# A hybrid attention and expert layer: mixed heads transposed before the addition of x1, squares of x1 behind the copies of its transpose, zero rows of the biases written later

## What is computed

```
h = rms_norm(x, g_attn);  proj = h @ w_in
y_a = sparse attention, 8 heads of 64, over the 128 keys that an indexer picks
y_b = differential attention, 4 heads of 128, each normalised and scaled
x1  = x + concat(y_a, y_b) @ w_o
h2  = rms_norm(x1, g_ffn)
out = x1 + moe(h2)      # 4 of 32 experts for each token: gate/up, clamped SwiGLU, down
```

## Time and profile before

| | |
|---|---|
| time, median of 3 runs | 1516.82 us (1516.62 to 1521.65) |
| time of the profiled execution | 1517.85 us |
| its span, first to last instruction | 1515.7 us |
| mean granted clock of TensorE | 0.985 |
| PE busy | 1455.6 us, 96% |
| DVE busy | 1313.3 us, 87% |
| ACT busy | 1106.0 us, 73% |
| POOL busy | 235.3 us, 16% |

### The profile page before, as it was taken

The page is one execution under the profiler, slowest core; times in us unless marked ns, Lnnn a source line. Parts: engine busy times, 40 slices in busy tenths (PEclk is TensorE's granted clock), DMA queues, the critical chain, the costliest instruction groups (busy, mean ns, idle before and its releaser), DMA issues.

```text
span 1515.7 us, 18818 instructions
## 1 busy us (share of the span) xinstructions
PE 1455.6 (96%) x7145; PEld 1197.8 (79%) x7148; DVE 1313.3 (87%) x1320; ACT 1106.0 (73%) x1197; POOL 235.3 (16%) x120
## 2 busy tenths in 40 slices
PE   6999888989999999999999999999999999999996
PEld 5887767776788888888888888888888888888885
DVE  5799776548799999999999999999999999999995
ACT  6666554445777787788877787888778778887773
POOL 1222000011111111211111112111111221111101
PEclk9999979999999999999999999999999999999998
DMA  5422111168999999999999999999999999999991
GB/s 159 139 70 56 42 43 42 45 245 314 334 366 359 373 370 369 363 378 364 369 367 376 367 372 368 375 371 364 356 369 374 361 371 368 368 367 363 382 362 34
DMA packets 102308, 448.53 MB, mean 296 GB/s; under 512 B 18497, under 2 KB 23617, under 8 KB 69377
## 3 DMA queue, kind: packets, MB, share of 16 engines
q1 hardware_dynamic: 89808, 428.32, 73.1%
q0 software_dynamic: 9792, 18.90, 5.1%
q10 hardware_dynamic: 2608, 0.01, 0.1%
HBM read 440.89 MB, written 23.07 MB: 306 GB/s over the span
## 4 chain that ended last, share of the span: by engine, by line
PE 84%; DVE 10%; ACT 2%; issue 2%; DMA 1%; POOL 1%; ACTq 0%; POOLq 0%; DVEq 0%
PE ps L1950 68%; PE ps L1712 2%; PE ps L1714 2%; PE ps L1713 2%; PE ps L1960 2%; PE ps L1919 2%; PE ps L1724 2%; PE ps L1911 2%; DVE work L1390 1%; DVE top L1389 1%; DVE nmax L1401 1%; PE ps L1815 1%; DVE W L570 1%; DMA out_dram<-ysb 1%; PE ps L1786 0%
## 5 line engine op out<-in xcount | busy, mean ns | idle before, releaser
L775 DVE TENSOR_TENSOR whl<-wraw,whl 128x2048 fp32r<-128x2048 f32 x384 | 865.8, 2288 | 84.5 <-ACT whl L770 77.7
L770 ACT ACTIVATE whl<-wraw 128x2048 fp32r<-128x2048 f32 x384 | 732.7, 1918 | 208.2 <-PE ps L1950 208.2
L1950 PE MATMUL ps<-whl,xT 128*128 128x512 f32 x3120 | 732.1, 392 | 1.6 <-issue 1.3
L1950 PEld LDWEIGHTS ps<-whl,xT 128*128 128x128 f32 x3120 | 581.7, 188 | 123.5 <-issue 2.0
L1950 PE MATMUL ps<-whl,aT 128*128 128x512 f32 x1488 | 346.1, 391 | 0.4 <-DVE whl L775 0.4
L1950 PEld LDWEIGHTS ps<-whl,aT 128*128 128x128 f32 x1488 | 276.9, 188 | 56.8 <-DVE whl L775 0.8
L939 POOL DMA_INDIRECT out_dram<-ysb,idx x32 | 100.3, 3135 | 453.6 <-ACT ysb L1224 440.2
L930 POOL DMA_INDIRECT xg<-h_rows,idx x32 | 88.4, 2762 | 471.2 <-DVE idx L1608 463.5
L1712 PE MATMUL ps<-W,HT 128*128 128x512 f32 (+1 forms) x184 | 71.9, 391 | 5.4 <-DVE W L570 4.4
L1714 PE MATMUL ps<-W,HT 128*128 128x512 f32 (+1 forms) x184 | 68.9, 374 | 0.0
L1713 PE MATMUL ps<-W,HT 128*128 128x512 f32 (+1 forms) x184 | 68.6, 373 | 0.0
(11 more groups left out here) (248 smaller groups left out, 1363.0 us busy)
## 6 DMA issues: line engine op xcount, KB each, us to landing
wraw<-in_w_gu_dram SPq DMA_DIRECT2D x256, 1024.0 KB, 8.0
wraw<-in_w_down_dram SPq DMA_DIRECT2D x128, 1024.0 KB, 7.2
WR<-in_w_in_dram SPq DMA_DIRECT2D x20, 512.0 KB, 3.7
WR<-in_w_o_dram SPq DMA_DIRECT2D x8, 512.0 KB, 3.7
xs<-in_x_dram SPq DMA_DIRECT2D x4, 512.0 KB, 7.8
WR<-in_x_dram SPq DMA_DIRECT2D x4, 512.0 KB, 3.6
out_dram<-WR SPq DMA_DIRECT2D x4, 512.0 KB, 2.6
h_rows<-WR SPq DMA_DIRECT2D x4, 512.0 KB, 2.6
```

Source lines behind the costliest of these rows:

```text
L770: act.activation(whl[:, n % HL, 0, :], wraw[n % RAW], ACT.Copy).then_inc(chunk_hi, 1)
L775: eng.tensor_tensor(whl[:, n % HL, 1, :], wraw[n % RAW], whl[:, n % HL, 0, :].bitcast(F32), ALU.subtract).then_inc(chunk_lo, 1)
L1950: ins = pe.matmul(bank, a[x_][j], w[:, b, j, 512 * q:512 * q + 512], start=c == NG and j == 0 and n == 0, stop=last and j == nj - 1 and n ...
```

## The change

Three things are altered. In the plan, both `turn_y` steps of tile 1 move from the end of unit 40 to the end of unit 39, ahead of `post(0)`; `turn_y(2, 1)` moves from unit 50 to unit 49, ahead of `post(1)`; and in unit 59 `post(2)` comes before `mix_b(3)`. On ACT the squares of x1 of tiles 0 to 2 move from `post` behind the copy in `turn_x1`. On POOL the zeros of the biases wait until both engines have read the bank of `turn_y(3, 1)`.

```
-        35: [("mix_b", 1)], 37: [("mix_scale", 1)], 40: [("turn_y", 1, 0), ("turn_y", 1, 1)],
-        44: [("mix_b", 2)], 46: [("mix_scale", 2)], 50: [("turn_y", 2, 1), ("mix_a", 2)], 53: [("turn_y", 2, 0)],
+        35: [("mix_b", 1)], 37: [("mix_scale", 1)], 39: [("turn_y", 1, 0), ("turn_y", 1, 1)],
+        44: [("mix_b", 2)], 46: [("mix_scale", 2)], 49: [("turn_y", 2, 1)], 50: [("mix_a", 2)], 53: [("turn_y", 2, 0)],
...
+LATE[59].reverse()
...
                 elif st[0] == "biases":
                     pool.wait_ge(score_ps, SCORE["all"])
+                    wait_turns(pool, through(("turn_y", T - 1, 1)))
...
                 elif kind == "post":
-                    t = st[1]
-                    if t < T - 1:
-                        act.wait_ge(x1_ok, t + 1)
-                        act.activation(h2, x1, ACT.Square, accum_out=tss[:, 0:1]).then_inc(x1_sq, 1)
+                    continue
                 elif kind == "turn_x1":
...
-                    if t == T - 1:
-                        act.wait_ge(x1_ok, T + 1)
-                        act.activation(h2, x1, ACT.Square, accum_out=tss[:, 0:1]).then_inc(x1_sq, 1)
+                    act.wait_ge(x1_ok, t + 1 if t < T - 1 else T + 1)
+                    act.activation(h2, x1, ACT.Square, accum_out=tss[:, 0:1]).then_inc(x1_sq, 1)
```

## The result

The changed kernel took 1511.26 us (median of 8 runs, 1509.66 to 1514.02). The kernel before, run again beside it, took 1519.9 us (8 runs, 1516.51 to 1524.14). The ratio is 0.9944, with a 95% interval of 0.9934 to 0.9955: 8.5 us, 0.56% less. The time lies 3.3 us above the forecast of 1508.0 and inside its range, close to its upper end. The gain itself, 8.5 us with an interval of 6.8 to 10.0, is 1 us short of the forecast sum of 9.5.

A forecast was written before the change was run, and what follows sets the result against it. TensorE is full in the experts, so its waits from 225 to 345 us and the half clock after them bound the gain. 2.45 + 0.2 + 2.65 + 2.5 + 1.7 = 9.5 us, forecast 1508.0 us, range 1505.5 to 1512.5.

The forecast's parts named there:

- Units 39 and 40: Heads of tile 1, x1 of tile 0: earlier transposes and out projection, with clock returning, give 2.45 us; bounds 0.75 to 2.6.
- rival (a): Clock gives nothing back after the pause before x1 of tile 0: 6.1 us remain, 1510.7; chance 0.25.
- Units 49 to 51: Tile 2's heads, x1 of tile 1: the wait only changes its name, 0.2 us; bounds 0.5 lost to 0.6 gained.
- Unit 59 and the squares: x1 of tile 2: earlier addition and later squares start the second half of transposes 2.65 us sooner; bounds 0.85 and 2.65.
- Rival (b): Only the zeros count; DVE's hold in `post_mean` and tile 1's late addition eat the rest: 4.2 us, 1512.6; chance 0.10.
- The zeros: Routing of tile 2: moving POOL's MEMSET frees DVE's held CAST and gives 2.5 us; bounds 2.2 and 2.5.
- The clock behind it: After the last out projection's shortened pause, half clock vanishes, giving 1.7 us; bounds 0 and 1.7.
- The base: Starting time of the forecast: profiled execution 1517.85 us, median of runs 1516.82; results 1508.3 and 1507.3, 1508.0 taken.
- Slower (c): After split pauses in units 39 to 41 the clock stays at 1.2 GHz, costing 12 us, 1519.5; chance 0.03.
- no effect (d): The moved MEMSET meets another row of DVE, at most 2.65 us; chance 0.04 together with others.

The follow-up runs named there:

- the kernel with the search put off: The changed kernel with DVE's top-k pairs of units 39 and 40 put off to the end of the search: 1508.86 us, ratio 0.9925.
- the kernel with the half head put back: The changed kernel with `turn_y(2, 1)` back in unit 50, behind the addition of x1 of tile 1: 1508.97 us, ratio 0.9929.
- all but the heads: The kernel before with the zeros later, unit 59 turned round and the squares behind the copies, without the moved `turn_y` steps: 1512.2 us, ratio 0.9948.
- the kernel with all three edits: The changed kernel with tile 1's `turn_y` in unit 38, top-k pairs of units 39 and 40 put off, `turn_y(2, 1)` back in unit 50: 1506.57 us, ratio 0.9907.

## Why the prediction came out as it did

**Units 39 and 40: the mechanism right, one part of the term wrong.** It had three parts. PE's transposes of x1 start sooner: the wait is named after the addition, as predicted. They were to start 2.4 us sooner and did so by 2.5 (237.61 less the 1.79 us lost ahead of unit 38 is 235.82, against 238.30). `turn_p` waits for DVE's copy and the out projection starts 1.5 us sooner: 241.85 less 1.79 is 240.06, 1.45 us. And then "if the clock is full again by then, [...] another 0.95". The clock was at half for as long and until as late as before, and of the 1.45 us 0.68 were left at unit 48. The bound that the prediction gave for this, "only the work that fits into 1.5 us of half clock is ahead, 0.75", is what happened; the term was 0.7 and not 2.45. The failed step is the reason given for the choice, "since PE now has work from 235.9 on instead of 238.3". That work is short, and the pause ahead of it is still 3.1 us, followed by a second of 1.7. The kernel with seven idle matmuls shows that the fall followed the first of them. That one and the kernel with the search put off, in which the first or the second pause was cut, had 3.4 us at half clock each; so both pauses seem to have a part in the 6.9 us. This was rival (a), for this stretch.

**Units 49 to 51: the sum right, its parts opposite.** 0.16 us against 0.2 predicted, and the wait did change its name. But the squares alone and the kernel with the half head put back show that the moved `turn_y` loses 0.27 us and that the squares give 0.43. The prediction reckoned only the sum of the links and did not see that the edit without the move would have been better.

**Unit 59 and the squares: right.** 2.55 us against 2.65, half from each edit (1.28 by the squares alone, 1.27 as the difference). DVE was held in `post_mean` for 1.77 us, 1.8 predicted, the row maximum behind it ran at 304.85, and no wait of PE followed from it. Rival (b), which let this hold eat the gain and leave 4.2 us, a ratio of 0.9972, is refuted by all but the heads, 0.9948 with an interval that ends at 0.9962.

**The zeros: right.** 2.49 us against 2.5, the CAST 0.17 us, PE's pause 1.07 against 1.3. The CAST took 2.67 us in all four traces that have the MEMSET beside it, and 0.17 in all ten that don't. At the new place the MEMSET, 2.66 us from 313.59, met no row of DVE: the last had ended at 313.38 and the next began at 318.70. The page SBUF — State Buffer of the Trainium skill, in its section Who interferes with whom, says that a cast on VectorE and an instruction on GpSimd can exclude each other on a shared port pair, the later one for the whole of the earlier. The trace agrees: both started within 0.01 us and ended within 0.03. That it is the port, no run here shows.

**The clock behind it: right in size for the profiled execution, too sure in its reason.** 1.6 us against 1.7. Every kernel that had the zeros moved took 34.71 to 34.73 us from unit 64 to the experts (ten executions). But the four traces that have the zeros in their old place took 36.33, 36.39, 37.07 and 37.74, behind the same pause of 3.56 us: two with 3.4 us at half clock and two with 6.8. So the upper bound of 1.7 was too low, and what the moved zeros give back is 1.6 to 3.0 us, 2.2 on average. That goes some way to explain why the medians say more than the traces, 5.0 us against 4.1 for the zeros alone. The reason given was that a pause of 2.1 us had left the clock as it was. In the kernel with the idle matmuls a pause of 2.10 us was followed by a fall, and in the changed kernel's second profile one of 1.50 was. None of the ten had a fall behind the 1.1 us ahead of unit 64, so the step held, but not for the reason given.

**The base.** The sum, with 0.7 in place of 2.45, is 7.75 us, and the trace's 7.5 agree. Taken from the profiled 1517.85 it gives 1510.1, beside 1510.59 measured. The forecast stood lower by the 1.75 us of the first term and by 0.3 us for the lower median of three runs, which the eight later runs did not bear out.

**What was luck.** The measured 1511.26 lies outside the 1506 to 1509.2 that had the chance of 0.58, and beside rival (a)'s 1510.7, whose gain of 6.1 us the measured 8.5 is not. It got there since the runs of before were 3.1 us slower than the three that the forecast started from. The 8.5 us come near the sum of 9.5 although a term of it was 1.75 too high: the medians show 1.0 more than the 7.5 of the traces, which their interval of 6.8 to 10.0 allows, and part of it may be the longer low stretches ahead of the experts. And the interval of the ratio was 0.1% to either side, so the change can be told from none, where the prediction asked for 0.5%.

**Slower (c) and no effect (d)** did not occur: the clock rose again 6.9 us after the fall, and the MEMSET met nothing.

## What to carry to other kernels

Where an engine waits for a queue, ask what stands in the queue and not only where the awaited instruction stands: `turn_y` moved up by one unit or two was worth 0.7 and 0.9 us there; with two of DVE's search pairs put off it was 3.3 and 5.6. Where a pause of TensorE is shortened and not removed, count no return of the clock in the likeliest case; here 4.8 us became 3.1 and 1.7 and the clock gave nothing. Cut both traces at the same instructions and compare lengths: that separated 0.3 us effects from executions that differ by up to 3.8 us in code that is the same (227.07 to 230.91 at unit 38).

## What the runs showed that I had not expected

**The fall of the clock is no fixed consequence of a pause.** In the experts there is a pause of 2.01 us ahead of the biases, in all fourteen traces at the same instruction; ten had a fall behind it and four had none. The kernel before, then the changed one:

```profile
382.06 1.16 PE L1960 MATMUL ps<-bgs,sel_gu 128*128 128x512 f32 x4 [2.01 <-DVE acts L1651]
383.16 4.61 PE L1950 MATMUL ps<-whl,xT 128*128 128x512 f32 x12
```

```profile
376.33 1.16 PE L1958 MATMUL ps<-bgs,sel_gu 128*128 128x512 f32 x4 [2.01 <-DVE acts L1649]
377.44 3.06 PE L1948 MATMUL ps<-whl,xT 128*128 128x512 f32 x12
```

The twelve products behind it took 4.61 us in one and 3.06 in the other. Pauses of 1.50 us (tile 1) and 2.01 us were followed by 3.4 us at 1.2 GHz in some executions and by none in others, the 2.14 us of before in tile 1 by none, the 2.10 us of the kernel with idle matmuls by 3.4, and one of 1.91, with 1.31 behind it, by 6.8. The pauses of 2.9 to 4.8 us in the places studied were followed by 3.4 to 6.9 us each time. In the first 60 us, too, executions of the same code had 3.4 to 10.2 us at half clock, and near 192 to 215 us, which no part of the change touches, 13.7 to 20.5, more than in all the places studied. What 3.4 us at half clock cost depends on the work in them: 1.6 us in these products and behind the zeros, 1.1 in tile 1, 0.3 in units 39 to 41, where PE waited for much of that time. The runs of one kernel differ by 1.5 to 8.6 us, so a few such stretches are a good part of it.

**The clock row doesn't show every low stretch.** In the kernel with all three edits the window below has a clock of 1.00, and its products take 0.63 us. In the same window the changed kernel has them at 0.63 with a clock of 0.52, and the kernel before at 0.39 with 1.00. The durations are the surer sign.

```profile
13.20:16.60 3.40, 3.40 (x10) 2.58 (x9) 3.40 (x5) 3.40 (x6) 0.00 (x0) 1.00 0.80 231
```

```profile
13.76 0.63 PE L1711 MATMUL ps<-W,HT 128*128 128x512 f32 x1
```

**What stays open.** The squares alone and the half head put back measured 2 to 2.5 us better than the rows of their traces account for. Stretches of half clock that come in one execution and not in another could be the cause; this was not tested. Nor is it shown what decides whether a pause of 1.5 to 2.1 us is followed by a fall.
